# Differential attention: the mix of the two softmax maps moved ahead of the new scores' maxima, with three banks for scores and one for values

## The reference, cut to what matters

```python
def one_block(q_blk):
    s = jnp.einsum('bqhmd,bkhmd->bhmqk', q_blk, k).astype(F32) * scale
    p = jax.nn.softmax(s, axis=-1)
    a = p[:, :, 0] - lam * p[:, :, 1]
    return jnp.einsum('bhqk,bkhe->bqhe', a.astype(v.dtype), v)
```

## Time and profile before

| what | value |
|---|---|
| median of 3 runs | 4074.11 us (4073.48 to 4078.53) |
| profiled execution, its own time | 4075.18 us |
| its span from first to last instruction | 4073.4 us |
| mean granted TensorE clock | 0.921 |
| TensorE matmul busy | 3520.0 us (86%) |
| VectorE busy | 2173.2 us (53%) |
| ScalarE busy | 1484.2 us (36%) |
| transposes of L1222, whole program | 688, TensorE idle before them 53.7 us |

### The profile page before, as it was taken

One profiled execution on the slowest core, in us unless ns is written; L12 is line 12 of the kernel. 1 busy time (PEld: TensorE's weight loads), 2 busy tenths in 40 slices (PEclk: granted clock), 3 DMA queues, 4 the chain that ended last, 5 costly groups with the idle time before them and its releaser, 6 DMA issues. The chain is left out here.

```text
span 4073.4 us, 48565 instructions
## 1 busy us (share of the span) xinstructions
PE 3520.0 (86%) x17656; PEld 2897.3 (71%) x17656; DVE 2173.2 (53%) x4168; ACT 1484.2 (36%) x2863; POOL 504.0 (12%) x398
## 2 busy tenths in 40 slices
PE   7887888878789999778879999889998779789998
PEld 6666667666577888556667888668887557667886
DVE  3565634656426775566665333336775666663333
ACT  3313333133424444333434332335443334344332
POOL 0000000000002322111021111002232110112110
PEclk9988889888899999889889999889999889899999
DMA  4620036311153221222223333343223212333332
GB/s 129 182 77 26 30 94 176 89 40 32 44 154 112 73 72 56 77 57 76 79 73 109 95 97 97 98 134 94 74 72 94 57 52 56 94 99 89 97 98 84
DMA packets 554596, 350.09 MB, mean 86 GB/s; under 512 B 73428, under 2 KB 497364, under 8 KB 554092
## 3 DMA queue, kind: packets, MB, share of 16 engines
q1 hardware_dynamic: 554348, 346.84, 30.1%
HBM read 301.36 MB, written 45.42 MB: 85 GB/s over the span
## 5 line engine op out<-in xcount | busy, mean ns | idle before, releaser
L631 PE MATMUL bank<-h,w_hi 128*128 128x512 f32 x2240 | 957.1, 427 | 173.8 <-DVE w_low L624 121.7
L632 PE MATMUL bank<-h,w_hi 128*128 128x512 f32 x2240 | 905.3, 404 | 0.0
L633 PE MATMUL bank<-h,w_low 128*128 128x512 f32 x2240 | 904.1, 404 | 0.0
L618 ACT CAST w_hi<-w 128x1024 fp32r<-128x1024 f32 (+2 forms) x456 | 432.8, 950 | 673.4 <-DMA w<-in_w_mlp 391.0
L624 DVE TENSOR_TENSOR w_low<-w,w_hi 128x1024 fp32r<-128x1024 f32 (+2 forms) x456 | 522.0, 1145 | 238.4 <-ACT w_hi L618 232.3
L631 PEld LDWEIGHTS bank<-h,w_hi 128*128 128x128 f32 x2240 | 438.5, 196 | 292.7 <-DVE w_low L624 162.4
L633 PEld LDWEIGHTS bank<-h,w_low 128*128 128x128 f32 x2240 | 436.9, 195 | 101.3
L632 PEld LDWEIGHTS bank<-h,w_hi 128*128 128x128 f32 x2240 | 439.1, 196 | 90.7 <-issue 9.8
L632 PE MATMUL bank<-yT_low,w_hi 128*128 128x512 f32 x768 | 312.5, 407 | 0.0
L1251 ACT ACTIVATE prob<-bank,softmax_stat 128x512 f32<-128x512 f32 (+3 forms) x256 | 144.9, 567 | 288.6 <-DVE softmax_stat L1283 222.7
L631 PE MATMUL bank<-yT_low,w_hi 128*128 128x512 f32 x384 | 166.5, 434 | 56.0 <-DVE xT L766 42.4
(11 more groups left out here) (426 smaller groups left out, 6048.6 us busy)
## 6 DMA issues: line engine op xcount, KB each, us to landing
w<-in_w_in SPq DMA_DIRECT2D x148, 512.0 KB, 4.2
w<-in_w_mlp SPq DMA_DIRECT2D x128, 512.0 KB, 4.0
z<-z_tile SPq DMA_DIRECT2D x164, 256.0 KB, 4.3
w<-in_w_gate SPq DMA_DIRECT2D x64, 512.0 KB, 4.1
q_twice<-z SPq DMA_DIRECT2D x128, 128.0 KB, 2.9
w<-in_w_branch SPq DMA_DIRECT2D x64, 256.0 KB, 2.9
k_twice<-z SPq DMA_DIRECT2D x88, 128.0 KB, 3.7
w<-in_w_out SPq DMA_DIRECT2D x32, 256.0 KB, 2.8
```

Source lines behind the costliest of these rows:

```text
L618: self.a.copy(self.wh[s][:, 0:d, 0:n], self.w[s][:, 0:d, 0:n]).then_inc(self.w_high.sem, 1)
L631: self.t.matmul(bank[0:n, :], wh, high, start=j == 0, stop=False)
L632: self.t.matmul(bank[0:n, :], wh, low, start=False, stop=False)
L633: return self.t.matmul(bank[0:n, :], wl, high, start=False, stop=j == self.depth(i) - 1)
```

## The change

`attend_dve` is changed for stages that mix (only `Diff` does): `scale_dve` of unit n-2 stands ahead of the maxima of unit n in VectorE's list, not behind them. `Diff` gets three banks for scores (0 to 2), banks 3 and 4 for transposes, and one bank (5) for values. Nothing is computed otherwise, and no instruction is added or removed; other users of `Attention` keep their order.

```diff
     def attend_dve(self, p, side=None):
         for new, turn, value in self.steps(p):
+            if turn is not None and self.mixes:
+                self.scale_dve(turn)
             if new is not None:
                 u = self.unit(new)
                 for m in range(self.maps):
@@
             if turn is not None:
-                self.scale_dve(turn)
+                if not self.mixes:
+                    self.scale_dve(turn)
                 if turn % 2 == 0:
@@
 class Diff(Attention, Rotation, NormedHeads):
     maps, mixes = 2, True
-    score_banks, other_banks, share = 2, ((2, 3), (4, 5)), 0.85
+    score_banks, other_banks, share = 3, ((3, 4), (5, 5)), 0.85
@@
         self.init_attention(8)
+        self.obank = [self.bank[5]]
         self.init_rotation(8, 4, ("rot2", "cos2", "sin2"))
```

## The result

The changed kernel takes 4012.02 us (median of 4 runs, 4008.35 to 4018.50) against 4074.06 us before (4 runs): a ratio of 0.9838, 95% interval 0.9819 to 0.9857, 62 us less. The forecast was 4028 with a range from 4013 to 4049, so the direction was right, and the gain was a third larger than the 46.6 us of the sum and just outside the range. The profiled execution took 4009.37 us, 1.8 us above its span.

The account below looks back on a forecast made before the run. TensorE, busy 86% of the span, was taken as the bound, its transposes waiting 53.5 us for VectorE's mix. Terms 55 - 12 + 1 - 1.4 - 1 + 5 gave 46.6 us gained, so 4028 us, range 4013 to 4049.

Parts of the forecast that it names:

- the sum: All terms over the four attention passes: 55 - 12 + 1 - 1.4 - 1 + 5 = 46.6 us gained, 1.1%.
- Clock: TensorE's slow clock in the passes: shorter pauses win back a quarter, 5 us, with ends of 0 and 20.
- What the move takes away: Transposes' waits for VectorE's mix, steps 2 to 7 of each pass: 24 waits of 2.3 us go, 55 us.
- what is late next: New waits for the mix in four exceptional cases: 3.3 us per first pass, 2.6 per second, 12 us come back.
- The step without a piece: Where no piece of the stream follows, about once a pass, the next transposes wait 0.9 us for the mix.
- the one behind a large low part: Where the stream's large low part lies between output and mix, about once a pass, the mix ends 0.6 us late.
- Banks: Third score bank gains 1 us (0 to 2.6); lone value bank loses 1.4 us where two units' values stand together.
- the rival: The clock comes back in full: all passes stay at 2.4 GHz after their start, 4014 to 4017; chance 0.21 for 4012 to 4022.
- VectorE did not become the bound: Rival: VectorE bounds every step, each of 24 keeps 1 to 1.2 us; 28 us gained, 4046; chance 0.20.
- Nothing was absorbed: Rival: stream fetches or second-pass rows come late and TensorE waits for transfers; 0 to 8 us gained, 4066 to 4075; chance 0.06.
- L309 did not wait in every step: Rival: the lone value bank makes values wait at L309 in every step; 35 us lost, 4109; chance 0.03.
- the clock case: Passes at full clock after their start, 4012 to 4022, chance 0.21; the range began at 4013, nearly at its end.

Follow-up runs that it names:

- the idle matmuls: Kernel before with one value bank, plus eight unread matmuls per step between scores and transposes, in 24 steps: 4060.33 us, ratio 0.9953 to the kernel before.
- order alone: Changed kernel with the old banks, two for scores and two for values, keeping VectorE's new order: 4018.57 us, ratio 0.9851 to the kernel before.
- banks alone: Changed kernel with VectorE's old order, keeping the new banks: 4078.99 us, ratio 1.0006 to the kernel before.
- the run with one value bank: Kernel before with a single value bank (5) and bank 4 unused, nothing else: 4076.74 us, ratio 0.9994 to the kernel before.
- pauses put back: Changed kernel whose transposes also wait for the exponential of the step's second map, in 24 steps: 4075.01 us, ratio 0.9994 to the kernel before.
- the mix made earlier: Changed kernel with unit n-1's mix in step n, behind maxima and copy, ahead of the output: 4002.32 us; with old banks 4001.15, then 4000.07 when repeated.

## Why the prediction was wrong

The mechanism was right, and one term was mis-sized: the step "Clock. ... I take a quarter, **5 us**". It measured 20 us, by the idle matmuls (20 to 22 by the time at 1.2 GHz). With 20 in place of 5 the sum is 61.6 us and the time 4013.6 against the profiled execution, 4012.5 against the median; measured were 4012.0. The other terms held to within 1 or 2 us each:

- *What the move takes away, less what is late next.* Without the clock the sum was 41.6 us. The passes' 62.4 less the clock's 20.1 are 42.3. I had 3.3 us of new waits in a first pass; recorded were 0.47, 0.29 (the second map of unit 3, waiting for its bank), 0.90 and 0.53 (behind the large low part), so 2.2, or some 2.8 with the 0.15 us that the record leaves out of each. For a second pass I had 2.6 and 0.5 at its end; recorded were 0.67, 0.51, 0.81 and 0.89. The step without a piece and the one behind a large low part stand where I had put them.
- *Banks.* The sum had a gain of 1 us for the third score bank and a loss of 1.4 for the lone value bank. The loss came: 0.8 us at the end of each first pass (recorded as a wait of 0.5), 1.6 in all, and only there, as argued. The gain did not: with and without the third bank the first passes are equal up to the last transposes. The 1.3 us of the earlier trace rows were misread. They are waits of the weight loads of L1211; its matmuls show none over 0.15 us in those two passes. Together order alone against the change says a loss of 1.3 us (181.0 to 182.3), banks alone a gain of 0.4 (244.7 to 244.3), in which the slow stretches lie in other places. The rule of the Trainium skill (Perfetto Trace Analysis, Optimizing Tensor Performance, Matmuls), by which every value would have paid, doesn't bind in this kernel: the run with one value bank is at 0.9994.
- *The clock.* I bounded it rightly (0 to 20 us) and then argued it down. The reason was a single stretch of full speed between two pauses, and that the passes begin slow. The first was no evidence for what happens with shorter pauses: in the same pass the clock was at 0.55 for the 10 us of 1702 to 1712, among equal pauses. The second was right and already taken out (12 of the 67 us). What remained was slow because of the pauses, nearly all of it, and the runs bear this out from both sides: idle matmuls in the pauses left 15 of 62 us at 1.2 GHz and gave 20 us, and pauses put back took the clock down again. My bound had the size right; the quarter had no row behind it. The rule of the Trainium skill that I had set beside the rival (TensorE: Matmul & The Clock Gate, Part 1), by which activity lifts the slow clock, agrees with these runs: two matmuls a step raised the passes from 0.84 and 0.91 to 0.94 and 1.00. I had set that rival at 0.21 with 4012 to 4022, and that is what came; of the signs that I had named, 0.85 to 0.92 for the forecast and 0.95 for this rival, the passes' 0.93 and 0.99 point to the rival.
- *The other rivals.* VectorE did not become the bound: the ordinary step lasts 3.63 us, with no wait before its transposes, and just as long with the mix made earlier. Nothing was absorbed: the passes' 62.4 us and the medians' 62.0 agree. L309 did not wait in every step, so the change was not slower.
- *The range.* Its low end followed from the clock case, "nearly to its end", and so cut off the case that came.

## What to carry to other kernels

When a wait of the busiest engine repeats every few microseconds, look at the order of the list of the engine that ends it: work whose inputs were ready a step ago belongs in front of work that waits for this step's results, or better still right behind the last step's. Price such a wait twice, once as idle time and once as the clock that it costs the matmuls around it; the granted clock by window gives the second, and if the pauses are its cause, take it in full. A bank more helps at most where the profile shows matmuls waiting for one: here a second value bank is worth 0.8 us in two passes of four, a third score bank nothing.

## What the runs showed that I had not expected

Two idle matmuls a step (48 in all four passes together, 0.46 us a step) in time that TensorE would have stood still were enough for the whole 20 us: passes of 227.6 against 247.7 us, with the pauses still 1.7 us long. The effect is not in proportion to what is filled; eight matmuls gave no more. And a kernel with as little of recorded waits as 0.9 us in the transposes still has a clock of 0.92 in its first passes, 7 us each at 1.2 GHz. They begin in one wait of 4.4 us ahead of the first scores, which no run here removed.
